# Gated linear attention with one state between tiles of 128 tokens, the chunk inside a tile handled by a block of the attention matrix

## The reference, cut to what matters

```python
def step(state, inp):                      # one chunk of 64 tokens, all heads
    qi, ki, vi, gi = inp
    bcum = jnp.cumsum(gi, axis=-2)
    b_last = bcum[..., -1:, :]
    q_dec = qf * jnp.exp(bcum)
    k_inv = kf * jnp.exp(-bcum)
    k_end = kf * jnp.exp(b_last - bcum)
    att = jnp.where(causal, einsum('bhcd,bhsd->bhcs', q_dec, k_inv), 0.0)
    o = einsum('bhcs,bhse->bhce', att, vf) + einsum('bhcd,bhde->bhce', q_dec, state)
    state = exp(b_last)[..., None] * state + einsum('bhcd,bhce->bhde', k_end, vf)
    return state, o
```

## Time and profile before

| | |
|---|---|
| median of 3 runs | 1638.78 us (1637.18 to 1639.89) |
| the profiled execution's own time | 1638.86 us |
| its span, first to last instruction | 1637.1 us |
| PE busy | 1564.2 us, 96% of the span |
| DVE busy | 519.2 us, 32% |
| ACT busy | 287.0 us, 18% |
| POOL busy | 74.8 us, 5% |
| mean granted clock of TensorE | 0.984 of full speed |

### The profile page before, as it was taken

The page is one execution under the profiler, slowest core; times in us unless marked ns, Lnnn a source line. Parts: engine busy times, 40 slices in busy tenths (PEclk is TensorE's granted clock), DMA queues, the critical chain, the costliest instruction groups (busy, mean ns, idle before and its releaser), DMA issues. The chain is left out here.

```text
span 1637.1 us, 21537 instructions
## 1 busy us (share of the span) xinstructions
PE 1564.2 (96%) x8781; PEld 930.2 (57%) x8781; DVE 519.2 (32%) x1080; ACT 287.0 (18%) x548; POOL 74.8 (5%) x109
## 2 busy tenths in 40 slices
PE   5999999899999999995999999998999999899997
PEld 2475654344434444432445588554888887588743
DVE  2444323111111111113210211122788888620000
ACT  2222101111111112111111020101222222320000
POOL 0000000000000000000000000001121221000000
PEclk9999999999999999998899999998999999999999
DMA  9444738799999999997142144234354443333440
GB/s 403 182 155 158 297 141 346 299 422 422 421 422 422 422 422 422 422 422 300 69 154 104 52 155 154 103 136 150 130 180 143 146 174 133 116 119 139 154 154 26
DMA packets 53740, 375.98 MB, mean 230 GB/s; under 512 B 7200, under 2 KB 18080, under 8 KB 19120
## 3 DMA queue, kind: packets, MB, share of 16 engines
q1 hardware_dynamic: 53392, 374.02, 57.7%
q10 hardware_dynamic: 288, 1.11, 0.2%
HBM read 373.99 MB, written 1.11 MB: 229 GB/s over the span
## 5 line engine op out<-in xcount | busy, mean ns | idle before, releaser
L1228 PE MATMUL ps<-ring,x_gathered 128*64 128x512 f32 x1024 | 225.2, 592 | 0.9 <-DVE x_gathered L1296 0.9
L1950 PE MATMUL ps<-hT,ring 128*128 128x256 f32 x768 | 172.4, 383 | 1.9 <-PEq L113 1.9
L1416 PE MATMUL ps<-ring,zT 128*128 128x512 f32 x384 | 165.6, 592 | 0.0
L1950 PEld LDWEIGHTS ps<-hT,ring 128*128 128x128 f32 x768 | 145.3, 192 | 23.5 <-issue 4.3
L1228 PEld LDWEIGHTS ps<-ring,x_gathered 128*64 128x64 f32 x1024 | 73.5, 137 | 146.6 <-issue 146.6
L1305 DVE TENSOR_TENSOR act_slots<-gate,ps 64x512 f32<-64x512 f32 x32 | 22.1, 690 | 378.6 <-ACT gate L1267 378.6
L1416 PEld LDWEIGHTS ps<-ring,zT 128*128 128x128 f32 x384 | 72.8, 190 | 89.9 <-issue 89.7
L1251 PE MATMUL ps<-ring,act_turned 128*64 128x512 f32 x512 | 116.9, 598 | 0.0
L1532 PE MATMUL ps<-hT,ring 128*128 128x256 f32 x512 | 111.9, 380 | 0.0
L2160 PE MATMUL ps<-uT,ring 128*128 128x256 f32 x512 | 111.0, 379 | 0.0
L1532 PEld LDWEIGHTS ps<-hT,ring 128*128 128x128 f32 x512 | 96.8, 190 | 16.0 <-issue 3.1
(11 more groups left out here) (466 smaller groups left out, 1604.8 us busy)
## 6 DMA issues: line engine op xcount, KB each, us to landing
ring<-in_experts SPq DMA_DIRECT2D x192, 1024.0 KB, 15.7
ring<-in_weights SPq DMA_DIRECT2D x75, 2048.0 KB, 8.1
b_raw<-in_s_b SPq DMA_DIRECT2D x16, 128.0 KB, 7.2
s_a_rows<-s_ab_rows SPq DMA_DIRECT2D x64, 32.0 KB, 6.5
c_raw<-in_s_c SPq DMA_DIRECT2D x16, 128.0 KB, 6.2
b_by_state<-in_s_b_by_state SPq DMA_DIRECT2D x16, 128.0 KB, 2.0
x<-in_x ACTq DMA_DIRECT2D x1, 1024.0 KB, 5.3
mix_room<-in_mem SPq DMA_DIRECT2D x1, 1024.0 KB, 15.1
```

What stands on the lines that cost most here:

```text
L1228: last = pe.matmul(h_ps[rows, :], xg[:, f, :], w[:, kk, m, :], start=(f == 0), stop=(f == KD - 1))
L1416: last = pe.matmul(self.bank(n, t), self.zT[:, 8 * kb + kk, t * P:(t + 1) * P], w[:, kk, :], start=(first and kk == 0), stop=(self.ends(i) ...
L1950: last = pe.matmul(out[:, f, :], w[:, kk, (2 * h + f) * P:(2 * h + f + 1) * P], rhs[:, kk, :], start=(kk == 0), stop=(kk == KD - 1))
```

## The change

Only one state remains, that between the two tiles. Inside a tile the second chunk takes the first chunk's part from a 64 by 64 block of `att`, which was zero before: k_end of the first chunk, transposed to `endT` by eight new transposes, times q of the second chunk (`cross_ps`, eight new matmul calls). For tile 1 the second chunk's q is then multiplied by the first chunk's decay, so that one product with the state serves all 128 tokens of the tile. The state is built from tile 0 alone, both chunks at once: two products per head, in two banks, the first one scaled by the second chunk's decay and the other added. The updates now stand ahead of `intra(0)`, and use banks 0 to 3 too, so `intra(0)` moves behind `half(12)` and waits for the states.

```diff
+        endT = sb("k_end_turned", [P, 4, TT, 64])
...
+        state_ps = lambda h: two((4, 0, 2, 4)[h])
+        endT_ps = k.ps[:, 4, :].rearrange("p (h t s) -> p h t s", h=4, t=TT)
+        cross_ps = k.ps[0:64, 0, :].rearrange("p (i s) -> p i s", i=8)
...
                 def intra(t):
                     for h in range(4):
-                        pe.matmul(lo[:, h, :], att[:, 2 * h + t, :], v[:, t, h * 512:(h + 1) * 512],
-                                  start=True, stop=False, skip_group_check=True)
-
-                def inter(t, c, stop):
+                        last = pe.matmul(lo[:, h, :], att[:, 2 * h + t, :], v[:, t, h * 512:(h + 1) * 512],
+                                         start=True, stop=(t == 0), skip_group_check=True)
+                    return last
+
+                def inter(t):
                     for h in range(4):
-                        pe.wait_ge(state_ready, 4 * (2 * t + c - 1) + h + 1)
-                        last = pe.matmul(lo[rows_of(c), h, :], qT[:, h, t * P + 64 * c:t * P + 64 * c + 64],
-                                         state[:, h, :], start=False, stop=stop, skip_group_check=True)
+                        last = pe.matmul(lo[:, h, :], qT[:, h, t * P:(t + 1) * P], state[:, h, :],
+                                         start=False, stop=True, skip_group_check=True)
                     return last
 
-                def update(t, c, hs):
-                    for h in hs:
-                        i = 4 * (2 * t + c) + h
-                        if i >= 2:
-                            pe.wait_ge(state_ready, i - 1)
-                        pe.matmul(k.ps[:, 4 + h % 2, :], key[rows_of(c), t, h * P:(h + 1) * P],
-                                  v[rows_of(c), t, h * 512:(h + 1) * 512], start=True, stop=True).then_inc(upd_done, 1)
+                def update(t, h):
+
+                    if h == 3:
+                        pe.wait_ge(state_ready, 1)
+                    for c in range(2):
+                        last = pe.matmul(state_ps(h)[:, c, :], key[rows_of(c), t, h * P:(h + 1) * P],
+                                         v[rows_of(c), t, h * 512:(h + 1) * 512], start=True, stop=True)
+                    last.then_inc(upd_done, 1)
...
                 turn(k, pe, ek, 4, fm(two(2)), turned)
+                for h in range(4):
+                    for t in range(TT):
+                        last = pe.transpose(endT_ps[:, h, t, :], key[0:64, t, h * P:(h + 1) * P], k.c("ident")[0:64, 0:64])
+                last.then_inc(turned, 1)
                 half(8)
...
+                for h in range(4):
+                    for t in range(TT):
+                        last = pe.matmul(cross_ps[:, 2 * h + t, :], endT[:, h, t, :], qT[:, h, t * P + 64:(t + 1) * P],
+                                         start=True, stop=True)
                 last.then_inc(att_done, 1)
...
-                intra(0)
-                update(0, 0, range(4))
+                for h in range(4):
+                    update(0, h)
                 half(12)
-                inter(0, 1, True)
-                update(0, 1, range(4))
-                pe.sem_inc(o_ready, 1)
+                pe.wait_ge(state_ready, 4)
+                intra(0).then_inc(o_ready, 1)
                 half(13)
                 pe.wait_ge(tile_out, 1)
                 intra(1)
-                inter(1, 0, False)
-                update(1, 0, range(4))
+                inter(1).then_inc(o_ready, 1)
                 half(14)
-                inter(1, 1, True).then_inc(o_ready, 1)
...
-                dve.wait_ge(turned, 8)
+                dve.wait_ge(turned, 9)
                 dve.tensor_copy(qT[:], fm(two(0)))
+                dve.tensor_copy(endT[:], endT_ps)
                 dve.tensor_copy(kT[:], fm(two(2))).then_inc(qkT_ready, 1)
...
-                                    k.ps[:, 4:6, :].rearrange("p b (i t) -> p (b i) t", i=4)).then_inc(att_ready, 1)
-                for t, c in ((0, 0), (0, 1), (1, 0)):
-                    for h in range(4):
...
+                                    k.ps[:, 4:6, :].rearrange("p b (i t) -> p (b i) t", i=4))
+                for h in range(4):
+                    dve.tensor_scalar(qT[:, h, 192:256], qT[:, h, 192:256], decay[:, 2 * (4 + h):2 * (4 + h) + 1], None, ALU.mult)
+                dve.drain()
+                dve.tensor_copy(att[0:64, :, 64:128], cross_ps).then_inc(att_ready, 1)
+                for h in range(5):
+                    if h < 4:
+                        dve.wait_ge(upd_done, h + 1)
+                        dve.tensor_scalar(state[:, h, :], state_ps(h)[:, 0, :], decay[:, 2 * h + 1:2 * h + 2], None, ALU.mult)
+                    if h:
+                        dve.tensor_tensor(state[:, h - 1, :], state[:, h - 1, :], state_ps(h - 1)[:, 1, :], ALU.add
+                                          ).then_inc(state_ready, 1)
                     dve.drain()
-                    if (t, c) == (0, 1):
-                        dve.wait_ge(o_ready, 1)
-                        dve.tensor_copy(v[:, 0, :].rearrange("p (h e) -> p h e", h=4), lo).then_inc(tile_out, 1)
+                dve.wait_ge(o_ready, 1)
+                dve.tensor_copy(v[:, 0, :].rearrange("p (h e) -> p h e", h=4), lo).then_inc(tile_out, 1)
```

## The result

| | before | after |
|---|---|---|
| median, same chip | 1637.98 us (1635.54 to 1639.89, 4 runs) | 1626.43 us (1625.46 to 1629.04, 4 runs) |
| ratio | | 0.9928, 95% interval 0.9913 to 0.9943 |
| profiled execution | 1638.86 us, span 1637.1 | 1625.46 us, span 1623.7 |
| mean granted clock | 0.984 | 0.985 |

The change makes the kernel 11.8 us faster by the ratio (9.3 to 14.3), 0.72%. The forecast was 11.9 us less.

What follows compares the result with a forecast made beforehand. PE's work was taken to bound the stretch: -7.15 - 3.87 - 3.2 + 2.3 = -11.9 us, so 1638.8 - 11.9 = 1626.9 us; own range 1625.5 to 1628.5, eight in ten 1624.3 to 1630.5.

Steps and rivals of the forecast that it cites:

- What goes: On PE, two inter blocks (7.15 us) and update(1,0) (3.87 us) go, counted in full.
- What is merged: On PE, update(0,0) and update(0,1), 7.70 us, become one block of alternating row halves, 4.5 us: 3.2 us less.
- The reading of `scatter`: Four scatter calls of the merged updates' form take 1.73 us, 0.87 a pair, so the two halves run side by side.
- the rival of pairs in sequence: Merged updates run one behind the other, saving only 0.6 us there: 1629.5 us in all, chance 0.14.
- The hold: Before the fourth update pair, PE waits for head 0's banks: start at 3.46 instead of 2.58 us, costing 0.9.
- What is added: On PE, eight transposes 0.5 us, cross block 1.3 and four seams 0.5: together 2.3 us, between 1.6 and 3.4.
- Hidden work: DVE's copies, scalings and state work stay covered by PE's halves; state 4 done by 8 us, wanted at 11.6.
- The rival of the state chain on DVE: DVE's state operations take 1.3 us instead of 0.7, delaying head 0; 1.2 us lost, 1628.1 us, chance 0.06.
- Weight tiles and clock: Two rivals: time given back at a weight load, 1638.8 us, chance 0.03; clock falls, say 1640.7 us, chance 0.03.
- The mis-sized term: Fewer tiling-mode changes on PE: most of their gain was taken as already in the subtracted starts, so nothing was added.
- The estimate of about 0.6 us: Six mode changes after against about eleven before, at 0.12 us each: some 0.6 us more off, not used.
- A sign of being wrong: The prediction is wrong if the lead at half(15), forecast some 12 us, is larger than at the span's end.

Runs made afterwards that it cites:

- the second comparison: The changed kernel run again unedited, against the kernel before: median 1624.89 us against 1639.0, ratio 0.9908 (0.9890 to 0.9926), 15.1 us less.
- e3: Changed kernel with the four calls of intra(1) issued three times instead of once: median 1631.09 us, 6.86 us more between the two marks.
- e1: Changed kernel with update products ordered first chunk of all heads, then second, head 0 in banks 6 and 7: median 1626.43 us, ratio 0.9932.
- v1: Changed kernel with head 0's products in banks 6 and 7, half(12) waiting instead of the fourth pair: median 1624.12 us, ratio 0.9920.
- e2: Changed kernel with the one inter cut into eight calls with 64 columns of weights, output halves by turns: median 1626.17 us, ratio 0.9935.
- e4: Changed kernel with update products ordered two lower rows, two upper, and again, head 0 in banks 6 and 7: one execution, 1627.22 us.

## Why the prediction was right

The range held the time, and the forecast, 11.9 us, meets the measured 11.8. That the two meet within 0.1 is luck: the second comparison gave 15.1. The stretch says more exactly 13.03, so the sum was 1.1 short. Its terms:

- *What goes* (7.15 + 3.87 us): as forecast. e3 shows that such calls count in full.
- *What is merged* (3.2 us): 7.70 - 4.48 = 3.22. The reading of `scatter` decided this; e1 confirms it, and the rival of pairs in sequence falls. The hold came where it was put, pair 3 at 3.43 us (forecast 3.46), and v1 shows that it was the wait for banks 4 and 5.
- *What is added* (2.3 us, 1.6 to 3.4): 2.1. Transposes 0.64 with seam 0.1 around, at the cheap end, as the row of the same shape said; the cross block 1.07, 0.067 a record, below the middle that I took. Seams and a little more on the halves around make up the rest: `half(8)` 6.97 against 6.87, the attention products 1.88 against 1.79, and 0.11 up to the updates.
- *Hidden work*: every cover held, with 3.9 us left before `qkT_ready` is wanted and 4.5 before state 4. The rival of the state chain on DVE falls: each operation took 0.68 to 0.75 us, and the chain ended 7.0 us behind the first update's start (forecast: by 8). One sum of that rival was too low: with operations of 1.3 us head 0 would be ready at 1.16 + 3 x 1.3 = 5.1, not 4.6, and 1.7 us would be lost, not 1.2. Nothing else hangs on it.
- *Weight tiles and clock*: no wait on a load, and the granted clock was 1.00 from 844 to 970 us. The 24 transposes in a row and the new hold did nothing to it.
- *The mis-sized term* is the one about the mode changes: "most of that already sits in the starts that I subtract, and I add nothing". It didn't. A seam also lies in the first or last call of the block that stays. `half(12)` went from 7.11 to 7.01 us, `half(13)` from 7.01 to 6.91, `intra(0)` from 3.60 to 3.44, `intra(1)` from 3.52 to 3.43, the `inter` that stays from 3.57 to 3.43, and the halves from 14 on are 0.31 shorter together. That is 0.90 us. With the 0.2 of the added work it is the whole gap of 1.1. The estimate of about 0.6 us, which the prediction made by the rule of the Trainium skill ("TensorEngine Tiling (Array Packing)", Key Properties) and did not use, had the right sign and two thirds of the size. e2 shows the cause: one stay in another mode put back, 0.34 us, in the same three places. `intra(0)` gained 0.16 us, more than one seam; it also no longer stands behind the wait for `v`, and no run separates the two.
- *A sign of being wrong*: the prediction named a lead at `half(15)` that is larger than at the end. It is: `half(15)` starts 935.02 - 921.13 = 13.9 us earlier, and the span is 13.4 shorter. The 0.5 us is lost behind the second mark, where executions with the same code differ by up to 3.1 us and PE's five longest waits are the same before and after within 0.1 us, so it doesn't show that the change gives time back.

## What to carry to other kernels

When products use half of the array's rows or columns, look for partners on the other half; it was worth 3.2 of 13 us here, nearly as much as a whole dropped block. The two products of a pair went to different banks in every run; what one bank for both would do, none shows. Count the changes of mode, and price them at the neighbours as well as at the block. Where a product waits for a bank, look for banks that nobody uses at that moment, and give them to the product that is read first: they are free again by the time their next user comes. Where two halves run side by side, mind the order for the signals too, as the next section shows.

## What the runs showed that was not expected

A matmul on free rows starts ahead of its place. The Trainium skill ("TensorE: Matmul & The Clock Gate", Part 3) says that matmuls start and end strictly in program order. By that rule the order of e4 (two lower, two upper, twice) has 13 record slots of 0.43 us, 5.6 us; it took 3.78 with its tail. The order of e1 has 15 slots, 6.4 us; it took 5.50. The windows of e1, for the update line alone, show how. A record is drawn longer (589 ns) than the 0.43 us to the next one on its rows, so one half of the array shows up to two active records in a window, and both halves show four. They show two at first, then four for about 1 us, then two again (columns: us, PE busy and count, PEld busy and count, clock, DMA share, GB/s).

```profile
886.61:886.82 0.21, 0.21 (x2) 0.16 (x1) 1.00 0.39 153
886.82:887.03 0.21, 0.21 (x3) 0.02 (x2) 1.00 0.76 306
887.47:887.68 0.21, 0.21 (x4) 0.21 (x2) 1.00 1.25 536
888.33:888.54 0.21, 0.21 (x4) 0.13 (x1) 1.00 0.54 230
888.75:888.97 0.21, 0.21 (x3) 0.13 (x1) 1.00 1.96 842
888.97:889.18 0.21, 0.21 (x2) 0.05 (x1) 1.00 0.54 230
```

How far ahead it reached can be read from the weight loads of e1. Up to 886.58 they come singly, 0.43 us apart; from 887.01 on they stand close together:

```profile
886.58 0.19 PEld L1557 LDWEIGHTS ps<-gla_v,gla_qk 64*128 64x128 f32 x1 [0.24 <-issue]
887.01 1.16 PEld L1557 LDWEIGHTS ps<-gla_v,gla_qk 64*128 64x128 f32 x7 [0.24 <-issue]
```

887.01 is 1.82 us behind the first load, and by the records it is where the third call on the lower rows starts. So the first call on the upper rows, the fifth in the program, started beside the third: two places ahead, and not sooner, although its rows were free from the beginning. In e4 every upper call stands two places behind the lower one that it can run beside, and all of them overlapped. Whether the limit counts calls, records or something else, no run shows.

The signals did not run ahead. By e1's records the first upper product ends 2.95 us behind the first load, but its step of `upd_done` comes at 3.73, 0.03 behind the end of the last lower product (3.70); in e4 it ends at 1.17, and its step comes at 2.01, behind the second lower product (1.98). So a product that started ahead of its place was reported in its place, and DVE started its first scaling at 3.75 and 2.04 us, all counted from the first load. That is the late first state of e1 and e4, and it is why strict alternation, where each product is reported within 0.02 us of its end, is the better order.

Not expected either: `half(0)` takes 7.1 us in two of the nine profiled executions (after and after_again) and 8.8 in the other seven, at a granted clock of 1.00 and 0.83 between 784 and 794 us, with the same code up to there; this alone moves a profiled span by 1.7 us.
